# Layer A's prologue with the memory's rows first, its residual turned from raw rows, and norm weights loaded as rows

## The reference

```python
def layer_a(x, mem, ln_g, w_in, mem_ln_g, w_mem, w_out):
    h = rms_norm(x, ln_g)
    z = h @ w_in
    ...
    y_mem = memory_attention(q_mem, rms_norm(mem, mem_ln_g), w_mem)
    y = jnp.concatenate([y_mix, y_mem], axis=-1) * jax.nn.silu(gate)
    return x + y @ w_out
```

## Time and profile before

| | |
|---|---|
| time, median of 3 runs | 2216.1 us (2212.26 to 2218.34) |
| the profiled execution | 2220.56 us, span 2218.9 us, granted clock 0.965 |
| PE busy | 2072.7 us (93%), 10092 instructions |
| DVE busy | 1148.4 us (52%) |
| ACT busy | 826.1 us (37%) |
| POOL busy | 401.3 us (18%) |
| DMA | 160.07 MB, mean 72 GB/s |

### The profile page before, as it was taken

The page is one execution under the profiler, slowest core; times in us unless marked ns, Lnnn a source line. Parts: engine busy times, 40 slices in busy tenths (PEclk is TensorE's granted clock), DMA queues, the critical chain, the costliest instruction groups (busy, mean ns, idle before and its releaser), DMA issues. The chain is left out here.

```text
span 2218.9 us, 28775 instructions
## 1 busy us (share of the span) xinstructions
PE 2072.7 (93%) x10092; PEld 1687.3 (76%) x10092; DVE 1148.4 (52%) x2029; ACT 826.1 (37%) x1487; POOL 401.3 (18%) x343
## 2 busy tenths in 40 slices
PE   3899999999999999999998998999999986998998
PEld 2468878888878878888886786788777875886786
DVE  4636364555546363636444424576768684333423
ACT  3434343434334343534333312444444442333310
POOL 2123222232323232323210013101010101000010
PEclk6899999999999999999999999999999988999998
DMA  8222211221221212221313522210101012222512
GB/s 252 77 66 55 74 50 57 62 66 56 58 61 48 76 48 61 57 71 48 129 44 90 186 66 104 63 39 20 58 19 57 19 38 81 67 57 73 183 57 95
DMA packets 211553, 160.07 MB, mean 72 GB/s; under 512 B 8705, under 2 KB 196385, under 8 KB 210978
## 3 DMA queue, kind: packets, MB, share of 16 engines
q1 hardware_dynamic: 203762, 145.06, 21.9%
q0 software_dynamic: 4928, 8.70, 1.6%
q10 hardware_dynamic: 2800, 5.51, 0.7%
HBM read 130.56 MB, written 28.67 MB: 72 GB/s over the span
## 5 line engine op out<-in xcount | busy, mean ns | idle before, releaser
L283 DVE TENSOR_TENSOR w_lo<-w_raw,w_hi 128x512 fp32r<-128x512 f32 x303 | 266.1, 879 | 348.9 <-ACT w_hi L279 348.3
L207 PE MATMUL z_ps<-b_parts,w_hi 128*128 128x512 f32 x656 | 267.4, 408 | 13.7 <-ACT g_gate L217 5.5
L279 ACT ACTIVATE w_hi<-w_raw 128x512 fp32r<-128x512 f32 x308 | 192.7, 626 | 224.0 <-PE z_ps L312 100.9
L209 PE MATMUL z_ps<-b_parts,w_lo 128*128 128x512 f32 x656 | 261.8, 399 | 0.0
L310 PE MATMUL z_ps<-ah_hi,w_hi 128*128 128x512 f32 x608 | 247.3, 407 | 5.1 <-PEq L1887 4.3
L312 PE MATMUL z_ps<-ah_hi,w_lo 128*128 128x512 f32 x608 | 241.5, 397 | 0.0
L311 PE MATMUL z_ps<-ah_lo,w_hi 128*128 128x512 f32 x608 | 240.9, 396 | 0.0
L208 PE MATMUL z_ps<-b_parts,w_hi 128*128 128x512 f32 x560 | 224.4, 401 | 0.0
L207 PEld LDWEIGHTS z_ps<-b_parts,w_hi 128*128 128x128 f32 x656 | 125.8, 192 | 47.4 <-issue 19.5
L192 DVE TENSOR_TENSOR w_lo<-w_raw,w_hi 128x1024 fp32r<-128x1024 f32 (+1 forms) x57 | 88.9, 1560 | 118.3 <-ACT w_hi L188 117.8
L209 PEld LDWEIGHTS z_ps<-b_parts,w_lo 128*128 128x128 f32 x656 | 125.8, 192 | 29.8
(11 more groups left out here) (401 smaller groups left out, 4120.7 us busy)
## 6 DMA issues: line engine op xcount, KB each, us to landing
w_raw<-in_a_win SPq DMA_DIRECT2D x220, 256.0 KB, 3.0
w_raw<-in_b_win SPq DMA_DIRECT2D x33, 512.0 KB, 4.1
y_scratch<-y SPq DMA_DIRECT2D x16, 512.0 KB, 3.0
w_raw<-in_a_wout SPq DMA_DIRECT2D x8, 768.0 KB, 5.8
w_raw<-in_b_wout SPq DMA_DIRECT2D x8, 768.0 KB, 6.2
xt_scratch<-work ACTq DMA_DIRECT2D x2, 2048.0 KB, 10.3
ares<-xt_scratch POOLq DMA_DIRECT2D x8, 512.0 KB, 3.8
y<-y_scratch SPq DMA_DIRECT2D x8, 512.0 KB, 4.2
```

The source lines that it names most:

```text
L207: pe.matmul(z_ps[s][:, 0:width], w_hi[slot][:, k, :], hi[k][:, tok], start=(k == 0), stop=False)
L209: mm = pe.matmul(z_ps[s][:, 0:width], w_lo[slot][:, k, :], hi[k][:, tok], start=False, stop=(k == nk - 1))
L279: act.activation(op_ring(w_hi, u), op_raw[i], ACT.Copy).then_inc(hi_op, 1)
L283: eng.tensor_tensor(op_ring(w_lo, u), op_raw[i], op_ring(w_hi, u).bitcast(F32), ALU.subtract).then_inc(lo_op, 1)
```

## The change

Three things. (1) The norm weights come as rows: six DMAs on ACT's queue put 42 rows of 128 values into a spare diagonal buffer; PE transposes them once, DVE copies them to `gains` and `onorm`. (2) The 4 blocks of the memory are taken first, then the 8 of x. Keys are made in halves between the turning of x; the scaled memory goes to buffers of its own (`mg`), keys into `z_ps`; products start after all keys; the orders on ACT and DVE are new. x is no longer stored to `xt_scratch`. (3) The residual of layer A: SP loads x as raw rows (two DMAs of 2 MB) during memory attention, PE turns them there in 16 blocks of 4 transposes, ACT and DVE move them into `xb`, and the output projection adds its product to that in place.

```diff
...
+            gain_rows = [(A[n] if n == "lnf" else A[n][0]).rearrange("(k p) -> k p", p=P)
+                         for n in ("a_ln", "a_mln", "b_ln", "b_mln", "lnf", "b_onorm")]
...
+            srcs = [(A[n][0], i) for n in ("mem_prompt", "mem_sample") for i in range(NMEM // P)]
+            srcs += [(A[n][0], i) for n in ("x_prompt", "x_sample") for i in range(SEQ // P)]
...
+                def key_weights(h):
+                    sp.dma_start(wk[h], w_view(A["a_wmem"][0], h * HD)).then_inc(wk_in[h], 16)
                 sp.dma_start(ident[:], A["c_ident"]).then_inc(ident_in, 16)
-                for t in range(NT):
+                for t in range(NM):
                     row(t)
+                key_weights(0)
+                for t in range(NM, N):
+                    row(t)
+                    if t == NM + 3:
+                        key_weights(1)
                 pair_load(sp, A["a_win"][0], (0, DIL_W), 0)
-                for t in range(NT, N):
-                    row(t)
-                for h in range(MEM_HEADS):
-                    sp.dma_start(wk[h], w_view(A["a_wmem"][0], h * HD)).then_inc(wk_in[h], 16)
+                key_weights(2)
+                key_weights(3)
                 for b in range(2):
-                    sp.wait_ge(moved[b], N)
+                    sp.wait_ge(moved[b], NM)
                 sp.dma_start(mt_scratch, mt).then_inc(mt_stored, 16)
                 pair_load(sp, A["a_win"][0], (3 * DIL_W, 4 * DIL_W), 1)
                 for b in range(2):
                     sp.wait_ge(kv_out[b], 16 * (3 - b))
+                sp.wait_ge(mt_stored, 16)
...
-                for i, n in enumerate(("a_ln", "a_mln", "b_ln", "b_mln", "lnf")):
-                    g = A[n] if n == "lnf" else A[n][0]
-                    pool.dma_start(gains[:, i, :], g.rearrange("(k p) -> p k", p=P)).then_inc(const_in, 16)
-                pool.dma_start(onorm[:], A["b_onorm"][0].rearrange("(k p) -> p k", p=P)).then_inc(const_in, 16)
...
+                def keys(h, half):
+                    if half == 0:
+                        pe.wait_ge(wk_in[h], 16)
+                    if half == 0 and h == 0:
+                        pe.wait_ge(gains_moved, 2)
+                    if half == 0 and h == 1:
+                        pe.wait_ge(mg_done, KC)
+                        pe.wait_ge(kv_moved, 1)
+                    if half == 0 and h > 1:
+                        pe.wait_ge(kv_moved, h)
+                    for k in range(4 * half, 4 * half + 4):
                         if h == 0:
                             pe.wait_ge(mg_done, k + 1)
-                        mm = pe.matmul(out[:, 0:MT], wk[h][:, k, :], mt[:, k, :], start=(k == 0), stop=(k == KC - 1))
-                    mm.then_inc(kv_done, 1)
+                        mm = pe.matmul(z_ps[h % 2][:], wk[h][:, k, :], mg[k // 4][:, k % 4, :], start=(k == 0),
+                                       stop=(k == KC - 1))
+                    if half == 1:
+                        mm.then_inc(kv_done, 1)
                 pe.wait_ge(ident_in, 16)
...
+                pe.wait_ge(const_in, 16 * 6)
+                pe.transpose(z_ps[0][:, 0:NGR], diag[0:NGR, NT - 1, :], ident[0:NGR, 0:NGR]).then_inc(gains_turned, 1)
+                for m in range(NM):
+                    pe.wait_ge(diag_done, m + 1)
+                    pe.matmul(z_ps[1][:, m * P:(m + 1) * P], ones[:], diag[:, m, :], start=True, stop=True).then_inc(m_row_done, 1)
+                turn(4)
+                turn(5)
+                keys(0, 0)
                 turn(6)
                 turn(7)
+                keys(0, 1)
+                turn(8)
+                spread(0)
+                turn(9)
+                keys(1, 0)
+                turn(10)
+                turn(11)
+                keys(1, 1)
+                keys(2, 0)
                 spread(1)
+                keys(2, 1)
+                keys(3, 0)
+                keys(3, 1)
+                pe.wait_ge(kv_moved, MEM_HEADS)
                 one(0)
-                for t in range(NT, N):
-                    turn(t)
-                for m in range(NM):
-                    pe.wait_ge(diag_done, NT + m + 1)
-                    pe.matmul(z_ps[1][:, m * P:(m + 1) * P], ones[:], diag[:, m, :], start=True, stop=True).then_inc(m_row_done, 1)
                 for b in range(2):
                     pe.wait_ge(moved[b], N)
                 for i in range(1, OPS):
...
-                def store(s):
-                    for b in range(2):
-                        act.wait_ge(moved[b], 4 * s + 4)
-                    tok = slice(s * SEQ, (s + 1) * SEQ)
-                    act.dma_start(xt_scratch[:, :, tok], xa[:, :, tok]).then_inc(x_stored_half[s], 16)
...
+                for i, g in enumerate(gain_rows):
+                    act.dma_start(diag[i * KC:i * KC + g.shape[0], NT - 1, :], g).then_inc(const_in, 16)
                 act.preload_act_table_set("natural_log_exp_and_others")
-                for t in range(5):
+                for t in range(NM):
                     row(t)
                 start(0)
...
+                row(4)
                 act.wait_ge(m_row_done, NM)
                 out(0, z_ps[1][:], m_row_scratch)
+                row(5)
+                row(6)
+                row(7)
+                start(1)
+                row(8)
+                row(9)
+                keys_out(0)
+                row(10)
+                row(11)
+                start(2)
+                high(0)
+                op_split_hi(act, 0, 0, 0)
+                high(1)
+                op_split_hi(act, 0, 1, 1)
+                keys_out(1)
+                op_split_hi(act, 0, 2, 2)
                 high(2)
+                op_split_hi(act, 0, 3, 3)
+                high(3)
                 op_split_hi(act, 0, 4, 4)
+                high(4)
+                keys_out(2)
+                keys_out(3)
+                high(5)
+                evict_act(act, qkv, 0, 0, 0, True)
+                op_split_hi(act, 0, 5, 5)
+                high(6)
                 evict_act(act, qkv, 0, 0, 1, True)
...
+                op_split_hi(act, 0, 6, 6)
                 evict_act(act, qkv, 0, 0, 2, True)
...
+                for i in range(4):
                     op_split_hi(act, 1, i, 7 + i)
...
+                def memory_rows(ks):
                     dve.wait_ge(kv_moved, 1)
-                    dve.wait_ge(mt_stored, 16)
-                    for k in range(KC):
-                        dve.scalar_tensor_tensor(out=mt[:, k, :], in0=mt[:, k, :], scalar=gains[:, 1, k:k + 1], in1=z_ps[1][:],
-                                                 op0=ALU.mult, op1=ALU.mult).then_inc(mg_done, 1)
+                    for b in range(2):
+                        dve.wait_ge(moved[b], NM)
+                    for k in ks:
+                        dve.scalar_tensor_tensor(out=mg[k // 4][:, k % 4, :], in0=mt[:, k, :], scalar=gains[:, 1, k:k + 1],
+                                                 in1=z_ps[1][:], op0=ALU.mult, op1=ALU.mult).then_inc(mg_done, 1)
                 dve.memset(eps_col[:], EPS).then_inc(eps_set, 1)
-                for t in range(4):
+                for t in range(NM):
                     row(t)
+                dve.wait_ge(gains_turned, 1)
+                dve.tensor_copy(gains[:].rearrange("p a k -> p (a k)"), z_ps[0][:, 0:5 * KC]).then_inc(gains_moved, 1)
+                dve.tensor_copy(onorm[:], z_ps[0][:, 5 * KC:NGR]).then_inc(gains_moved, 1)
+                dve.wait_ge(gains_moved, 2)
                 variance(0)
+                refine(0)
                 row(4)
-                refine(0)
                 row(5)
+                memory_rows(range(0, 4))
                 row(6)
-                dve.wait_ge(const_in, 16 * 6)
-                scale(0, 0)
+                memory_rows(range(4, KC))
                 row(7)
                 variance(1)
+                row(8)
+                refine(1)
+                row(9)
+                scale(0, 0)
+                row(10)
+                row(11)
+                variance(2)
+                scale(1, 0)
+                refine(2)
                 lows(0)
-                refine(1)
-                scale(1, 0)
                 scale(0, 1)
                 sums_of(1)
-                lows(5)
-                variance(2)
+                lows(1)
                 scale(1, 1)
-                refine(2)
-                lows(1)
                 sums_of(2)
                 lows(2)
-                memory_rows()
                 lows(3)
                 sums_of(4)
                 lows(4)
+                lows(5)
                 sums_of(6)
-                evict_dve(dve, qkv, 0, 0, 3, True)
+                lows(6)
                 dve.wait_ge(lo_op, RING)
                 op_split_lo(dve, 0, 5, 5)
+                evict_dve(dve, qkv, 0, 0, 3, True)
+                op_split_lo(dve, 0, 6, 6)
                 evict_dve(dve, qkv, 0, 0, 4, True)
-                op_split_lo(dve, 0, 6, 6)
-                lows(6)
```

(118 more changed lines are left out.)

83 lines of the change are left out of this document (33 added, 50 removed).

## The result

The changed kernel takes 2199.23 us in the median of 11 runs (2188.68 to 2207.47), the kernel before 2214.76 (2207.6 to 2219.72); the ratio is 0.994, interval 0.9924 to 0.9956: 9.7 to 16.8 us less. The forecast was 2191, range 2183 to 2204, faster. One timed run of this case, 2394.56 us at a granted clock of 0.813 where all others had 0.963 to 0.979, is left out of every comparison.

The account below looks back on a forecast made before the run. Bound: stretches where PE stands or runs slowly, chiefly the prologue's wait for norm weights. -31.3 (prologue) - 2.5 (clock) + 8.1 (turning x) + 0.7 (value weights) = -25.0, so 2216.1 becomes 2191.1; own range 2186 to 2197, with rivals 2183 to 2204.

Parts of the forecast that it names:

- rival A: Prologue's interleaved part: half clock lengthens the path to the last square by 12 us, total 2203; chance 0.18.
- The weights' rows land before the fourth memory row is turned: Prologue start: norm weights, loaded as rows by ACT, arrive by about 11.3 us, with 0 us of waiting.
- Rival C: Prologue: weights' rows come no sooner, PE's turn of them stands until 36.6, 25.3 later; total 2216; chance 0.03.
- Last variance at 41.8: Prologue: the last square and variance, after all rows are turned, are done at 41.8 us; DVE is the bound from there.
- The stores of x go, at no gain of their own: Prologue: dropping the 4 MB of stores to scratch gains nothing itself, as only DMA engines carried them.
- DVE's chain of 26.4 with 2 of contention: Prologue after 41.8: DVE's scales, refinement, diagonals, lows and differences set the pace; POOL beside them adds 2, bounds 0 and 3.4.
- The gate of `one(0)` behind high(4): Prologue's first product waits for ACT's copy of keys(2), queued behind high(4): high part and copy take 1.6.
- Next stage at 94.8: Prologue's end: the stage after it starts at 94.8 against 126.09, a gain of 31.3 us.
- Clock kept, -2.5: Start of the stage after the prologue: PE idles 0.9 instead of 4.27 us and keeps its clock, -2.5.
- Tail +8.1 and 0.7: End of layer A's memory attention: turning x costs +8.1; PE waiting for head 3's value weights behind x rows costs 0.7.
- D: PE at half clock becomes the prologue's bound, ending it at 127.5; slower, total 2226; chance 0.04.
- B: Cheaper all round: x hides in PE's gaps (+4.6), no contention (-2), keys(0) at full clock (-1.6), weights in time (-0.7): 2183; chance 0.13.

Follow-up runs that it names:

- the second median: The changed kernel unaltered, run again for a second profile and more times: 2194.93 us, ratio 0.9931 to the kernel before.
- the version with columns: The changed kernel with norm weights loaded as single words by POOL's six DMAs again, instead of rows: ratio 0.995 to the kernel before.
- The thinned version: The changed kernel with POOL's sums 2 to 4 of the first pair made for one of 128 weight columns; executed once for the trace, next stage at 95.42.

## Why the prediction was right

The waits that it named are the ones that went, and the new ones that it named came; two sizes in its sum were off. That the time lies in the range is in part luck. The forecast's own range was 2186 to 2197, and 2199.23 lies above it, in the part that was added for rival A (2203), whose half clock did not occur; the second median, 2194.93, lies inside. And the last variance, 2.5 us early, made up for part of a contention that was taken 6 us too low.

- *The weights' rows land before the fourth memory row is turned*: yes, 11.19. Rival C is out, and the version with columns shows what it would have cost, 11, not 25, as DVE waited to 27.45 and not to 36.6.
- *Last variance at 41.8*: 39.3. The first half of keys took 3.67 at full clock, from 18.94, where I had let it end at 24.5. Rival A fell with it; clock 1.00 up to 50 in both profiles of the changed kernel.
- *The stores of x go, at no gain of their own*: wrong in the new order. With them kept the next stage came at 102.04, 3.7 to 3.9 later, and DVE waited 2.7 us for them before it could scale x in place. So of the 28 us the rows' form gives 11.1 to 13.0 and the missing stores up to 3.9; the remaining 11 to 13 would be the new order's, which no run has alone. The walk through the new prologue had no store in it, so the forecast time does not suffer from this; what is wrong is where the gain was said to come from.
- *DVE's chain of 26.4 with 2 of contention*: mis-sized. The lengthened steps ahead of the first product sum to 1.1 + 2.0 + 2.1 + 1.8 + 1.1 = 8.1; I had the row (1.22 for 0.16) and took 2 from a bound of 3.4 that I had summed over four lengthened steps of the old order. Even that bound was too low. The thinned version shows the cause for the diagonals and the first low part (3.2 of the 8.1); for the three other steps it is argued from what POOL does in the same time. The first product came at 75.09 for 72.1, and not 6 late, as the last variance had come 2.5 early.
- *The gate of `one(0)` behind high(4)*: right as a mechanism (the copy at 74.46 releases it). Taking it away brings the first product 14 us sooner, but the next stage only 0.6, and 3.7 once the evictions are moved too.
- *Next stage at 94.8*: 98.1 to 98.3. From the first product to it 23.3 us, 22.7 forecast; so it is late by what the first product is late.
- *Clock kept, -2.5*: yes as a mechanism, 0.69 us of idle and then matmuls 0.23 apart at once. In the time of dilated attention it can't be told from the spread.
- *Tail +8.1 and 0.7*: 8.4 to 8.7, by the steps given: the last moves follow DVE's weight split. Head 3's weights were 14.9 us in landing and PE waited 0.40 and 0.63 for them. They were issued behind 4 MB of the same queue and came behind it. The Trainium skill's page "DMA: Bandwidth & Descriptors", section "Queues, rings and completion order", says that each DMA engine takes the descriptors of one queue in ring order. The trace agrees: 14.9 to landing for the 4.8 of before, and 14.3 for the last x rows, which were issued just ahead.
- *Sum*: -25.0 forecast; -19.3 from the two columns that the change moves, with 2.5 for the clock -21.8; -15.5 and -16.3 in the medians (intervals 9.7 to 16.8 and 10.4 to 19.9 less). The 3 us between -25.0 and -21.8 are the contention. The 3 to 6 us between those columns and the medians stay open: -19.3 lies outside the first interval and inside the second, and single profiles, which differ by 13 and 8 us in the stages that nobody changed, can't place them.
- *D* did not occur: PE had full clock in the keys up to 50. *B*'s hidden tail (+4.6) is out too; the one part of B that came is keys(0) at full clock.

## What to carry to other kernels

When a wait at the start is taken away, work out what sets the end of the stage behind it and what runs beside that engine from then on; here five of DVE's steps beside POOL's work grew by 8.1 us in all, and taking POOL away from two of them brought 2.7 to 2.9 at the stage's end, nearly as much as the best order of ACT's queue. Look for every release that is queued on one engine behind unrelated work: freeing one (copies of keys) brought 0.6 us at the stage's end, and 3.7 once the next (evictions) was freed as well. And price each part of a compound change alone: here the rows and the new prologue gained and the third part, turning x a second time to save its store, cost 8.4 to 8.7 for the 3.7 to 3.9 that it saved.

## What the runs showed of the hardware that I had not expected

- DVE's step over 4 elements, usually 0.16 us, takes 1.26 beside a POOL operation of 1.26, while a low part twice as long as that operation goes from 2.35 to 4.50: the small step is slowed eightfold, the large one less than twofold, as if it waited for about one POOL operation at a time. What exactly they wait for was not tried by itself.
- Two rows limit this. DVE's scalings, whose factor is read from a PSUM bank, are not lengthened: 2.72 beside two POOL steps, 2.71 without (at 51.11). And POOL can be the one that waits: in the version with norm weights as rows alone a POOL split of usually 1.3 us took 5.83, from 53.79, while two pairs of DVE steps beside it kept their 2.36 each; with the residual alone the same, 5.83 from 66.14. The scaling, and POOL's steps beside it, in the changed kernel's timeline:

```profile
57.78 3.02 POOL L283 TENSOR_TENSOR w_lo<-w_raw,w_hi 128x512 fp32r<-128x512 f32 x2 [7.67 <-ACT w_hi L279]
...
58.36 2.72 DVE L703 SCALAR_TENSOR_TENSOR work<-work,gains,v_ps 128x512 f32<-128x512 f32 x4
```

- PE's stands of 7.6 and 6.8 us dropped the granted clock to 0.50, those of 3.06 and 1.53 in the turning part did not. The kernel before had stood 2.07 us before 14.73, at the longest, turned one row in 1.09, and turned the next row, at 17.86, in 1.86; its granted clock from 15 to 20 was 0.66. What tells the two apart no run here shows.
